# Stick-breaking attention: masks as a product into PSUM, residual additions and key copies on GpSimd, and a new order of VectorE's work

## The reference, cut to what matters

```python
mask = s_pos < t_pos                                   # strictly earlier keys
log_stay = jnp.where(mask, jax.nn.log_sigmoid(-logits), 0.0)
log_beta = jax.nn.log_sigmoid(logits)
later = lax.cumsum(log_stay, axis=3, reverse=True) - log_stay
w = jnp.where(mask, jnp.exp(log_beta + later), 0.0)
out = jnp.einsum("bhqk,bhkd->bhqd", w, vb)
...
h = h + y_all @ w_out          # y_all = [rmsnorm(y_ssd), rmsnorm(o)]
```

## Time and profile before

| | us |
|---|---|
| median of 3 runs | 2126.75 (2126.26 to 2127.61) |
| the profiled execution | 2119.47 |
| its span, first to last instruction | 2117.7 |
| TensorE busy | 2019.0 (95% of the span) |
| VectorE busy | 1064.5 (50%) |
| ScalarE busy | 750.4 (35%) |
| GpSimd busy | 227.0 (11%) |
| granted TensorE clock, mean | 0.974 of full speed |

### The profile page before, as it was taken

The page is one execution under the profiler, slowest core; times in us unless marked ns, Lnnn a source line. Parts: engine busy times, 40 slices in busy tenths (PEclk is TensorE's granted clock), DMA queues, the critical chain, the costliest instruction groups (busy, mean ns, idle before and its releaser), DMA issues.

```text
span 2117.7 us, 28559 instructions
## 1 busy us (share of the span) xinstructions
PE 2019.0 (95%) x11514; PEld 1727.5 (82%) x11514; DVE 1064.5 (50%) x1388; ACT 750.4 (35%) x947; POOL 227.0 (11%) x191
## 2 busy tenths in 40 slices
PE   7999888999999999999899999999997899999996
PEld 6778656688888887999899999999885588888885
DVE  6668755544444554121543434345797543443434
ACT  4448734532231434223332122224434442222122
POOL 2011011200000130012200000002145120000001
PEclk9999999999999999999999999999998999999998
DMA  4225111122222221111122222222121022222221
GB/s 171 100 80 99 73 40 60 60 100 99 96 84 100 89 90 60 60 60 41 60 80 99 90 90 94 86 97 85 71 85 61 15 85 100 99 82 96 99 99 60
DMA packets 27792, 174.68 MB, mean 82 GB/s; under 512 B 4385, under 2 KB 4513, under 8 KB 7730
## 3 DMA queue, kind: packets, MB, share of 16 engines
q1 hardware_dynamic: 25680, 167.32, 21.8%
q0 software_dynamic: 1856, 5.90, 1.6%
q10 hardware_dynamic: 162, 0.10, 0.0%
HBM read 168.53 MB, written 4.78 MB: 82 GB/s over the span
## 4 chain that ended last, share of the span: by engine, by line
PE 68%; issue 20%; DVE 6%; ACT 4%; POOL 2%; DMA 1%; SPq 0%; POOLq 0%; DVEq 0%; ACTq 0%
PE lin L447 56%; PE aux L2171 1%; POOL squares L628 1%; PE aux L1283 1%; ACT w_hi L362 1%; PE aux L1740 1%; PE aux L1754 1%; DVE w_lo L369 1%; PE lin L1238 1%; PE lin L2141 1%; PE aux L2155 1%; DMA w_raw<-in_weights 1%; PE aux L1267 1%; PE aux L1768 1%; PE aux L2019 0%
## 5 line engine op out<-in xcount | busy, mean ns | idle before, releaser
L447 PE MATMUL lin<-v_hi,w_hi 128*128 128x264 f32 (+1 forms) x1712 | 573.8, 335 | 4.9 <-DVE v_lo L613 3.4
L447 PE MATMUL lin<-v_hi,w_lo 128*128 128x264 f32 (+1 forms) x1712 | 570.8, 333 | 0.0
L447 PE MATMUL lin<-v_lo,w_hi 128*128 128x264 f32 (+1 forms) x1712 | 569.4, 333 | 0.0
L447 PE MATMUL lin<-x_hi,w_hi 128*128 128x512 f32 (+1 forms) x1176 | 416.6, 354 | 17.7 <-DVE tmp L541 6.6
L369 DVE TENSOR_TENSOR w_lo<-w_raw,w_hi 128x2048 fp32r<-128x2048 f32 (+1 forms) x144 | 328.4, 2281 | 188.8 <-ACT w_hi L362 188.6
L447 PE MATMUL lin<-x_hi,w_lo 128*128 128x512 f32 (+1 forms) x1176 | 413.1, 351 | 0.0
L447 PE MATMUL lin<-x_lo,w_hi 128*128 128x512 f32 (+1 forms) x1176 | 412.5, 351 | 0.0
L362 ACT ACTIVATE w_hi<-w_raw 128x2048 fp32r<-128x2048 f32 (+1 forms) x155 | 292.9, 1890 | 286.1 <-PE lin L447 274.4
L447 PEld LDWEIGHTS lin<-v_hi,w_hi 128*128 128x128 f32 x1712 | 324.4, 189 | 40.5 <-DVE v_lo L613 4.4
L447 PEld LDWEIGHTS lin<-v_lo,w_hi 128*128 128x128 f32 x1712 | 324.3, 189 | 33.6 <-issue 0.7
L447 PEld LDWEIGHTS lin<-v_hi,w_lo 128*128 128x128 f32 x1712 | 324.2, 189 | 32.1
(11 more groups left out here) (373 smaller groups left out, 2353.1 us busy)
## 6 DMA issues: line engine op xcount, KB each, us to landing
w_raw<-in_weights SPq DMA_DIRECT2D x155, 1024.0 KB, 4.8
rel_by_distance<-tmp POOLq DMA_DIRECT2D x1, 2620.0 KB, 57.3
rel_bias<-rel_by_distance POOLq DMA_DIRECT2D x8, 264.0 KB, 2.9
h<-in_x_t SPq DMA_DIRECT2D x4, 512.0 KB, 8.1
out_t<-h SPq DMA_DIRECT2D x4, 512.0 KB, 2.8
o_t<-in_mem_t POOLq DMA_DIRECT2D x1, 1024.0 KB, 5.2
cst<-in_consts SPq DMA_DIRECT2D x1, 512.0 KB, 9.7
col<-in_cols ACTq DMA_DIRECT2D x1, 67.0 KB, 5.7
```

Of the source, the lines that this page charges most:

```text
L447: last = nc.tensor.matmul(o, a, b, start=(k % (L.kc // k_banks) == 0 and p == 0), stop=((k + 1) % (L.kc // k_banks) == 0 and p == 2))
```

## The change

- The masks on VectorE (`masked`: two instructions on `stay` and two on `w_att` for each head) go. In their place TensorE adds the product of the identity and a constant 128x128 tile into each diagonal block of the logits: 0 where the key is strictly earlier, -2^100 elsewhere. That is one more matmul for each of four key blocks, 32 in all. The two constant tiles are rounded once by ScalarE (`sb_fixed`).
- The second copy of the keys (into the other half of the partitions) moves from ScalarE (L1177) to GpSimd, which copies from the first copy; the logits wait for it (`sb_other`).
- The additions into `h` move from VectorE (L1437) to GpSimd (`pool_mixed_add`), alternating between two `tmp` slots; VectorE only empties the fill bank, and waits for the addition of two tiles before.
- VectorE's order: `output` and `x_lo` come ahead of emptying `mixed(2hd-7)` or `memory_keys(hd)`, which is now done in the same pass, and `stay_low(hd+1)` comes last.

```diff
@@ sb_logits @@
             pe.wait_ge(sem("sb_lo"), hd + 1)
+            pe.wait_ge(sem("sb_other"), hd + 1)
...
                 nc.tensor.matmul(sb_bank(hd, j), sb_k[s][:, 0, keys], sb_q[s][:, qs],
                                  start=(j < 3), stop=False, skip_group_check=True)
+                nc.tensor.matmul(sb_bank(hd, j)[:, 0:P], sb_fixed[:, 0, :], sb_fixed[:, 1, :],
+                                 start=False, stop=False, skip_group_check=True)
@@ act_sb_hi, act_sb_first @@
-            nc.scalar.activation(sb_k[s][own, 0, :], k_t[own, t, :], ACT.Copy)
-            nc.scalar.activation(sb_k[s][other, 0, :], k_t[own, t, :], ACT.Copy).then_inc(sem("sb_hi"), 1)
+            nc.scalar.activation(sb_k[s][own, 0, :], k_t[own, t, :], ACT.Copy).then_inc(sem("sb_hi"), 1)
...
+            for x, name in enumerate(("ident", "drop_upto")):
+                nc.scalar.activation(sb_fixed[:, x, :], const(name), ACT.Copy)
@@ new on GpSimd @@
+        def pool_sb_other(pool, hd):
+            own, other, s = sb_halves(hd)
+            pool.wait_ge(sem("sb_hi"), hd + 1)
+            nc.gpsimd.tensor_copy(sb_k[s][other, 0, :], sb_k[s][own, 0, :]).then_inc(sem("sb_other"), 1)
+            pool.wait_ge(sem("sb_other"), hd + 1)
+
+        def pool_mixed_add(pool, t):
+            pool.wait_ge(sem("fill_taken"), WA_FILL + t + 1)
+            nc.gpsimd.tensor_tensor(h[:, t, META:T2], h[:, t, META:T2], tmp[:, 2 + t % 2, 0:S1], ALU.add)\
+                .then_inc(sem("mixed_added"), 1)
@@ values @@
-                pe.wait_ge(sem("sb_w"), hd + 1)
+                pe.wait_ge(sem("sb_w_raw"), hd + 1)
@@ dve_stick: stays, mixed @@
-                link(dve, nc.vector.scalar_tensor_tensor(stay[:, :], sb_whole(hd), 0.0, stay_e[:, :], ALU.max, ALU.add))
-                masked(stay).then_inc(sem("sb_stay"), 1)
+                nc.vector.scalar_tensor_tensor(stay[:, :], sb_whole(hd), 0.0, stay_e[:, :], ALU.max, ALU.add)\
+                    .then_inc(sem("sb_stay"), 1)
...
+                if t >= 2:
+                    dve.wait_ge(sem("mixed_added"), t - 1)
                 dve.wait_ge(sem("fill_done"), p + 1)
-                nc.vector.tensor_tensor(part, fill_bank, rstd[:, 0:S1], ALU.mult).then_inc(sem("fill_taken"), 1)
-                dve.wait_ge(sem("fill_taken"), p + 1)
-                nc.vector.tensor_tensor(h[:, t, META:T2], h[:, t, META:T2], part, ALU.add)\
-                    .then_inc(sem("mixed_added"), 1)
-                dve.wait_ge(sem("mixed_added"), t + 1)
+                nc.vector.tensor_tensor(tmp[:, 2 + t % 2, 0:S1], fill_bank, rstd[:, 0:S1], ALU.mult)\
+                    .then_inc(sem("fill_taken"), 1)
@@ dve_stick: the loop @@
-                if hd in (1, 2):
-                    memory_keys(hd - 1)
-                if hd >= 5:
-                    mixed(2 * hd - 9)
...
-                weights_masked(hd)
+                if hd >= 2 and hd % 2 == 0:
+                    output(hd // 2 - 1)
+                if hd in (4, 5, 6):
+                    dve_operand(dve, l_sb, hd - 4)
+                if hd < 2:
+                    memory_keys(hd)
+                if hd >= 4:
+                    mixed(2 * hd - 7)
                 if hd < 7:
                     stay_low(hd + 1)
-                if hd >= 2 and hd % 2 == 0:
-                    output(hd // 2 - 1)
...
-                if hd in (4, 5, 6):
-                    dve_operand(dve, l_sb, hd - 4)
             output(3)
-            mixed(7)
             dve_operand(dve, l_sb, 3)
+            dve.wait_ge(sem("mixed_added"), KD)
@@ pool_stick, the tail of its order @@
             clear(l_sb, l_mem.idx + 1)
+            pool.wait_ge(sem("square_added"), l_sb.added0)
+            pool_sb_other(pool, 4)
+            pool_sb_other(pool, 5)
+            pool_sb_other(pool, 6)
+            pool_mixed_add(pool, 0)
             add_square(l_sb, 0)
+            pool_mixed_add(pool, 1)
+            pool.wait_ge(sem("mixed_added"), 2)
+            pool_sb_other(pool, 7)
+            pool_mixed_add(pool, 2)
             add_square(l_sb, 1)
+            pool_mixed_add(pool, 3)
+            pool_mixed_add(pool, 4)
             add_square(l_sb, 2)
+            pool_mixed_add(pool, 5)
+            pool_mixed_add(pool, 6)
+            pool_mixed_add(pool, 7)
             add_square(l_sb, 3)
```

More of the change, by code:

```diff
@@ L40 @@
 UNIT = 2048
-BIG = 3.0e38
+DROP = -(2.0 ** 100)
 NEG = -1.0e30
@@ L104 @@
            ("a_log", 1)]
-CONSTS = ["ident", "ones", "upper", "neg_tri", "neg_ones", "keep_after", "chunk_later", "chunk_of"]
+CONSTS = ["ident", "ones", "upper", "neg_tri", "neg_ones", "drop_upto", "chunk_later", "chunk_of"]
 def places(rows):
@@ L213, in build @@
         stay_lo = sb("stay_lo", [P, 1280], F32R, scope=phase)
-        sb("rest_of_conv_out", [P, S1], scope=phase)
+        sb_fixed = sb("sb_fixed", [P, 2, P], F32R, scope=phase)
+        sb("rest_of_conv_out", [P, S1 - 2 * P], scope=phase)
         q_t = sb("q_t", [P, 4, S1], scope=phase)
@@ L1387, in dve_stick @@
         def dve_stick(dve):
[L1388 to L1394, removed]
             def stays(hd):
@@ L1406, in stay_low @@
                     .then_inc(sem("sb_stay_lo"), 1)
-            def weights_masked(hd):
-                dve.wait_ge(sem("sb_w_raw"), hd + 1)
-                masked(w_att).then_inc(sem("sb_w"), 1)
             def output(t):
@@ L1430, in mixed @@
             def mixed(t):
-                p, part = WA_FILL + t, tmp[:, 3, 0:S1]
+                p = WA_FILL + t
                 if t == 0:
                     dve.wait_ge(sem("rel_kept"), 16)
+                if t >= 2:
+                    dve.wait_ge(sem("mixed_added"), t - 1)
                 dve.wait_ge(sem("fill_done"), p + 1)
-                nc.vector.tensor_tensor(part, fill_bank, rstd[:, 0:S1], ALU.mult).then_inc(sem("fill_taken"), 1)
-                dve.wait_ge(sem("fill_taken"), p + 1)
-                nc.vector.tensor_tensor(h[:, t, META:T2], h[:, t, META:T2], part, ALU.add)\
-                    .then_inc(sem("mixed_added"), 1)
-                dve.wait_ge(sem("mixed_added"), t + 1)
+                nc.vector.tensor_tensor(tmp[:, 2 + t % 2, 0:S1], fill_bank, rstd[:, 0:S1], ALU.mult)\
+                    .then_inc(sem("fill_taken"), 1)
             stays(0)
@@ L2351, in pool_stick @@
             pool.dma_start(rel_dram, rel_vec.unsqueeze(1).broadcast_to([8, P, VEC])).then_inc(sem("rel_kept"), 16)
+            pool_sb_other(pool, 0)
+            pool_sb_other(pool, 1)
             clear(l_ssd, l_mix.idx + 1)
+            pool.wait_ge(sem("square_added"), l_ssd.added0)
+            pool_sb_other(pool, 2)
             add_square(l_ssd, 0)
             add_square(l_ssd, 1)
+            pool.wait_ge(sem("square_added"), l_ssd.added0 + 2)
+            pool_sb_other(pool, 3)
             add_square(l_ssd, 2)
@@ L2657, in constants @@
         (r == c).astype(f), np.ones((P, P), f), (r <= c).astype(f), -(r >= c).astype(f),
-        -np.ones((P, P), f), np.where(r < c, f(BIG), f(0)), (same & (r > c)).astype(f),
+        -np.ones((P, P), f), np.where(r < c, f(0), f(DROP)), (same & (r > c)).astype(f),
         (r // 64 == c).astype(f)], 1)
```

## The result

The changed kernel takes 2113.15 us, median of 7 runs (2106.64 to 2118.05); beside it the kernel before took 2123.8 us (7 runs, 2120.15 to 2127.61, the three shown ahead among them). The ratio is 0.9945, 95% interval 0.9927 to 0.9962: 11.7 us faster, between 8 and 15.5 (the two medians differ by 10.65). In two of the later experiments one execution each (2848 and 3562 us, with a mean granted clock of 0.65 and 0.74) is left out of the median. Three quantities have to be kept apart here: the change's own gain, forecast at 10.3 us and measured at 11.7 (11.0 us between the two traces, from the first logits to the cross attention); the level, forecast at 2116.5 us from a median of three runs of before, 2126.75, that were all near the top of what this kernel shows; and the scatter, which is larger than either.

What follows compares the result with a forecast made beforehand. TensorE, busy 95% of the span, was taken to bound the kernel, with waits on VectorE's late bank emptying and the lowered clock. 10.1 - 0.2 + 0.4 = 10.3 us off 2126.75 gave 2116.5; range 2114.5 to 2118.5, wider 2113 to 2121.3.

Steps and rivals of the forecast that it cites:

- the level: Whole program: median 2116.5 us, from the earlier median of 2126.75 less a gain of 10.3.
- part 1: Heads 4 to 6, VectorE's new order: three periods from 48.9 to 38.1 us; 10.1 us gained after 0.7 for the clock.
- Part 2: Mask products in the logits: 0.29 us per head, bounds 0.24 and 0.44; net 0.2 us lost.
- 3 x 0.06 + 0.11 = 0.29: Mask products per head: three between longer products at 0.06 us, one between short ones at 0.11.
- Parts 3 and 4: Masks off VectorE, 13 us of its work, off the path or covered; key copies on GpSimd, 0.6 us each, worth 0.
- Part 4: Second key copies on GpSimd: 0.6 us each, over 5 us of slack before the logits, worth 0.
- Part 5: Additions on GpSimd, eight of 1.38 us: cost 0; the port lock meets `stay_low` and the splits, not `x_lo`.
- Part 6: End, from `values(7)` to the reciprocal: 0.4 us gained, bounds 0 and 0.43; most of a TensorE wait becomes a later one.
- 2.5 us or more added: Profile sign at the end: TensorE's wait before L447 gone, and this much added to its wait for L541.
- 1.5 us either way: Whole program: allowance for clock falls at other phases, from falls of 1.7 us each.
- the forecast's own range: Whole program: 2114.5 to 2118.5 us, from the bounds of the order, mask products and end; chance 0.65.
- the wider one: 2113 to 2121.3 us, adding rivals: port lock reaching the path (chance 0.13) and fewer clock falls (chance 0.10).

Runs made afterwards that it cites:

- the same shift: Two float32 products of 512 columns added ahead of the cross attention: 2113.64 us in the changed kernel, 2111.47 us in the kernel with the masks on VectorE.
- everything but the order: Changed kernel with VectorE's old order, keeping mask products, key copies and additions on GpSimd: 2122.52 us, ratio 0.9999 to the kernel before.

## Why the prediction was right, and where it was wrong

**What bounds, and part 1 (the order), right.** 10.8 us less 0.7 for the clock was forecast, 10.1; the three periods went from 48.9 to 38.6 us, 10.3. The idle before `mixed` was 0.18, 0.09 and 1.83 us against 0.15, 0.15 and 1.7. That the clock after head 6 falls or not was left open at 0 to 1.7 us, and it is open in fact: behind the same 1.83 us `mixed` took 3.0 us in the changed kernel's first two traces and 4.6 in its third.

**Part 2 (mask products), mis-sized in its terms.** The step "3 x 0.06 + 0.11 = 0.29" took the product's own time and left out the later weight load of the product behind it: 0.11 each, 0.42 to 0.44 us for each head, the upper bound. Against it the unit of weights landed 0.56 us earlier instead of 0.3 (213.40 against 213.96). Sum: 0.2 us gained instead of 0.2 lost, up to `exponents(4)`; that is luck in part, since the same kernel's third trace loses 0.7 there, by the low clock. The products' cost of 3.5 us over eight heads lies beside waits, as said, for all but heads 4 and 5.

**Parts 3 and 4, right in sum.** Nothing shows of either in the time. A GpSimd copy takes 0.61 us at the least and up to 1.5 beside VectorE, and no wait of TensorE for it exists. Part 4 was not quite "worth 0": without it TensorE waits 0.8 us longer for ScalarE in the first heads, by one trace.

**Part 5 (additions, and the port's lock), right.** `x_lo` took 0.75 us three times. The lock acts where the time order had it, on `stay_low`. In the changed kernel at head 6, timelines of VectorE and of GpSimd:

```profile
271.85 1.96 DVE L1413 TENSOR_TENSOR stay_lo<-stay,stay_hi 128x1280 fp32r<-128x1280 f32 x1
```

```profile
271.12 1.33 POOL L2350 TENSOR_TENSOR squares<-squares,tmp 128x512 f32<-128x512 f32 x1 [6.75 <-ACT tmp L609]
272.42 2.55 POOL L1202 TENSOR_TENSOR h<-h,tmp 128x512 f32<-128x512 f32 x1
```

`stay_lo` waits for the square and takes 1.96 us instead of 1.49; the addition waits until 273.8 for `stay_lo` and takes 2.55 instead of 1.28. That agrees with the rule cited in the prediction (the Trainium skill, SBUF — State Buffer, "SBUF: two separate sides"): each loser waits for the whole instruction of the other. TensorE needs `stay_lo` at 277.3. After head 4 the addition also stretches the low part of the queries (L1190) to 1.69 us from 0.69; nothing of TensorE waits for that either.

**Part 6 (the end), right in sum, wrong in a sign to look for.** The end gained 0.5 us for 0.4 forecast. The sentence "2.5 us or more added" to the wait for L541 was wrong by its own sum: 2.78 us instead of 2.08, so 0.7 added. Of the 1.5 us of idle taken away, 0.7 went into that wait and 0.3 into `w_out_b`'s own start. What it had not seen is that the clock, which had stayed up behind the 2.08 us, fell behind the 2.78:

```profile
296.00:298.00 2.00, 2.00 (x6) 1.58 (x5) 1.14 (x3) 1.24 (x2) 0.31 (x1) 0.50 0.00 0
```

In sum it cost nothing that shows: from the product behind this wait to the cross attention it is 49.0 us in both kernels, as later waits were shorter (3.67 us for 4.03, and two small ones gone).

**The level, wrong.** The step that failed is the term 2126.75 in the sum: "the median of the runs is 2126.75, 7.3 us above it; I take the difference as unchanged". It was the median of three runs between 2126.3 and 2127.6. With four more it was 2123.8, and in the later sets 83 runs of the same kernel lie between 2114.0 and 2128.2, median 2121.8; the three were near the top, as the profiled execution of 2119.47 us beside them hinted. From 2123.8 the same sum gives 2113.5, 0.4 us off the measured 2113.15: of the 3.4 us by which the forecast was too high, 3.0 are the level. The second step that failed is "1.5 us either way" for the clock elsewhere. The changed kernel's own 17 runs span 2106.6 to 2118.1, so neither the forecast's own range from 2114.5 (its bounds add up to 2115.1 to 2118.7) nor the wider one from 2113.0 had room for that; 2113.15 lies outside the first and at the very edge of the second. What the runs show in place of the 1.5 us: the shortest of the 17 had a mean granted clock of 0.978, the longest 0.972. In the traces a fall of the clock costs some 1.6 us. In the attention of block 2 the clock was low in four stretches in the trace before and in two in the shortest (82.2 us); in the changed stage too a fall comes in one execution and not in the next. Why the first three runs of before were all long stays open.

**What stays open.** The kernel with the masks on VectorE is 6 us faster than the changed one in two sets of runs on one chip, and 2.2 us with the same shift on another, and its stage is not shorter. In its traces the difference to the changed kernel lies mostly in falls of the clock in stages whose code is the same. Whether it is the rhythm of TensorE's work ahead of them, the arrival time, the chip or chance, these runs do not settle.

## What to carry to other kernels

When one buffer stands between two engines, look at what its reader has queued ahead of emptying it: here moving one instruction of 1.5 us (`stay_low`) behind `x_lo` and the emptying was worth over 11 of the 12 us, and taking some 19 us of work off the same engine (masks and additions) was worth nothing that shows. Before taking work off an engine, follow the chain that ends last through its queue and put the edit there; the next link is then the one to read (here ScalarE's `x_hi`, and behind it `w_out_b`'s root). And a forecast of a level needs the scatter of the executions: ask first how far runs of the unchanged kernel lie apart, and whether the profiled one sits at their middle.

## What the runs showed of the hardware

- The clock of TensorE after the same wait is not the same in each execution: behind 1.83 us of idle it stayed at the full level in two traces of one kernel and fell to half in the third, for 1.6 us of loss; behind the first wait of `w_out_b` for VectorE it stayed up in the kernel before (2.08 us) and fell in the changed one (2.78); behind 3.2 us in the cross attention it fell in one trace (30.1 us, clock 0.83) and not in another (25.9 us, 1.00). Behind waits of 1.9 us it did not fall in the trace of everything but the order.
- Executions of one kernel differ by 11 to 14 us of 2120, more than most single edits to it, and the mean granted clock goes with the time (0.978 in the changed kernel's shortest run, 2106.6 us; 0.972 in its longest, 2118.1).
- A product of 128 columns between longer ones costs TensorE 0.11 us, not its own 0.06, as the product behind it starts 0.05 us late.
- Between GpSimd and VectorE a two-input instruction of either waits for the other's end: an addition of 128x512 took 1.28 us alone and 2.55 behind `stay_lo`, and `stay_lo` 1.96 instead of 1.49 behind the square.
